# A two-block transformer layer in float32 on one core: the low part of the three weight sums of the feed-forward input made by an accumulating DMA

## The reference, cut to what matters

```
D_MODEL = 2048
SEQ = 256
D_FF = -(-8 * D_MODEL // (3 * 256)) * 256
...
        h = rms_norm(x, norm_ffn[l])
        gate_up = jnp.einsum('btd,df->btf', h, w_ffn_in[l])
        ff_gate, ff_up = jnp.split(gate_up, 2, axis=-1)
        x = x + jnp.einsum('btf,fd->btd', jax.nn.silu(ff_gate) * ff_up, w_ffn_out[l])
```

## Time and profile before

| | us |
|---|---|
| median of 3 runs | 2148.68 |
| lowest, highest | 2147.15, 2149.55 |
| span of the profiled execution | 2146.8 |
| shortest run less that span | 0.35 |
| median less that span | 1.9 |
| TensorE busy | 2135.6 (99%) |
| VectorE busy | 1742.5 (81%) |
| ScalarE busy | 1261.2 (59%) |
| GpSimd busy | 138.1 (6%) |

### The profile page before, as it was taken

One profiled execution on the slowest core, in us unless ns is written; L12 is line 12 of the kernel. 1 busy time (PEld: TensorE's weight loads), 2 busy tenths in 40 slices (PEclk: granted clock), 3 DMA queues, 4 the chain that ended last, 5 costly groups with the idle time before them and its releaser, 6 DMA issues.

```text
span 2146.8 us, 30208 instructions
## 1 busy us (share of the span) xinstructions
PE 2135.6 (99%) x10176; PEld 1788.8 (83%) x10176; DVE 1742.5 (81%) x2125; ACT 1261.2 (59%) x1483; POOL 138.1 (6%) x218
## 2 busy tenths in 40 slices
PE   9999999999999999999999999999999999999998
PEld 9988888888888888888888888888888888888886
DVE  6578788666565698999899887787889999999886
ACT  6465455465544665555555555557667666666565
POOL 2022433101000000000000000000000000000000
PEclk9999999999999999999999999999999999999999
DMA  7666555575555566666666666666666666656664
GB/s 254 182 189 211 157 157 150 174 236 174 183 186 181 186 205 199 198 196 198 203 188 196 200 193 199 192 204 187 206 206 187 188 193 194 193 180 208 203 193 152
DMA packets 211513, 412.35 MB, mean 192 GB/s; under 512 B 13176, under 2 KB 13280, under 8 KB 211296
## 3 DMA queue, kind: packets, MB, share of 16 engines
q1 hardware_dynamic: 208608, 402.70, 60.9%
q0 software_dynamic: 1920, 5.31, 0.8%
q10 hardware_dynamic: 896, 3.15, 0.5%
HBM read 409.01 MB, written 3.16 MB: 192 GB/s over the span
## 4 chain that ended last, share of the span: by engine, by line
PE 96%; DVE 2%; DMA 1%; ACT 0%; issue 0%; DVEq 0%; SPq 0%; ACTq 0%
PE gp L1983 49%; PE gp L1915 33%; PE mx L1983 10%; PE mx L2226 1%; PE mx L2110 1%; DVE w_lo L1194 1%; DMA raw<-a_w_out_in 1%; PE mx L2275 1%; DVE t_lo L1426 0%; DVE ff_lo L1193 0%; PE mx L2113 0%; DMA x_tok<-x_in 0%; PE mx L2107 0%; PE mx L2162 0%; PE mx L2206 0%
## 5 line engine op out<-in xcount | busy, mean ns | idle before, releaser
L615 ACT ACTIVATE w_hi<-raw 128x1024 fp32r<-128x1024 f32 x759 | 797.1, 1056 | 681.6 <-PE gp L1915 246.3
L1194 DVE TENSOR_TENSOR w_lo<-raw,w_hi 128x1024 fp32r<-128x1024 f32 x759 | 921.2, 1230 | 233.8 <-ACT w_hi L615 224.1
L1983 PE MATMUL gp<-w_hi,a_hi 128*128 128x512 f32 x1053 | 413.3, 393 | 0.0
L1983 PE MATMUL gp<-w_lo,a_hi 128*128 128x512 f32 x1053 | 410.1, 389 | 0.0
L1983 PE MATMUL gp<-w_hi,a_lo 128*128 128x512 f32 x1053 | 409.8, 389 | 0.0
L1983 PEld LDWEIGHTS gp<-w_hi,a_hi 128*128 128x128 f32 x1053 | 197.7, 188 | 43.0 <-issue 2.9
L1983 PEld LDWEIGHTS gp<-w_lo,a_hi 128*128 128x128 f32 x1053 | 197.6, 188 | 41.4
L1983 PEld LDWEIGHTS gp<-w_hi,a_lo 128*128 128x128 f32 x1053 | 197.8, 188 | 39.8
L1915 PE MATMUL gp<-w_hi,a_hi 128*128 128x512 f32 x576 | 229.9, 399 | 0.0
L1915 PE MATMUL gp<-w_lo,a_hi 128*128 128x512 f32 x576 | 224.6, 390 | 0.0
L1915 PE MATMUL gp<-w_hi,a_lo 128*128 128x512 f32 x576 | 224.3, 389 | 0.0
(11 more groups left out here) (420 smaller groups left out, 3305.3 us busy)
## 6 DMA issues: line engine op xcount, KB each, us to landing
raw<-a_w_in_in SPq DMA_DIRECT2D x192, 512.0 KB, 4.5
raw<-w_ffn_in_in SPq DMA_DIRECT2D x176, 512.0 KB, 4.5
raw<-w_in_in SPq DMA_DIRECT2D x175, 512.0 KB, 3.9
raw<-w_ffn_out_in SPq DMA_DIRECT2D x88, 512.0 KB, 4.6
raw<-a_w_out_in SPq DMA_DIRECT2D x64, 512.0 KB, 4.9
raw<-w_out_in SPq DMA_DIRECT2D x32, 512.0 KB, 4.0
raw<-w_proj_a_in SPq DMA_DIRECT2D x16, 512.0 KB, 4.6
raw<-w_proj_b_in SPq DMA_DIRECT2D x16, 512.0 KB, 4.7
```

The source lines that it names most:

```text
L615: act.activation(w_hi[:, slot], raw[:, slot], ACT.Copy).then_inc(hi_ready, 1)
L1194: dve.tensor_tensor(w_lo[:, slot], raw[:, slot], w_hi[:, slot], ALU.subtract).then_inc(lo_ready, 1)
L1983: ins = pe.matmul(out_, stat[sp_], mov[mp], start=start and p == 0, stop=stop and p == 2, skip_group_check=True)
```

## The change

In stage FFN_IN alone, VectorE no longer writes `t_lo`. ScalarE writes the negated high part into `t_lo` with a second activation behind `t_hi` (Copy with scale -1). GpSimd waits for it and issues one DMA from `t_sum` to `t_lo` that adds to what the destination holds: `t_lo` = -high + sum. It does so 32 times, on the semaphore `t_added`. TensorE's wait before the last nine matmuls, and VectorE's before it overwrites `t_sum`, are on `t_added` in this stage. The other stages keep their subtraction; `lows` only corrects their counts. No transfer is issued by hand elsewhere, and the shapes stay.

```diff
@@ -429,6 +431,18 @@
+        added_pairs = len(MIXED_FIRST) + (S[FFN_IN].steps - 1) * len(MIXED)
+
+        def added(i, n):
+
+            if isinstance(i, int) and i == 0:
+                return 16 * n
+            return i * (16 * len(MIXED)) + 16 * (n + len(MIXED_FIRST) - len(MIXED))
+
+        def lows(k, i, n):
+
+            return pairs(k, i, n - (added_pairs if k > FFN_IN else 0))
+
@@ -587,6 +601,9 @@
             pool.dma_start(ws_raw[:], a_w_s.rearrange("g p q -> p g q")).then_inc(ws_in, 16)
+            for n in range(added_pairs):
+                pool.wait_ge(t_neg_ready, n + 1)
+                pool.dma_start(t_lo[:].bitcast(F32), t_sum[:], accum_op=ALU.add).then_inc(t_added, 16)
             pool.wait_ge(ws_turned, 1)
@@ -744,6 +761,8 @@
                     act.activation(t_of(k)[1][:], t_of(k)[0][:], ACT.Copy).then_inc(t_hi_ready, 1)
+                    if k == FFN_IN:
+                        act.activation(t_lo[:], t_sum[:], ACT.Copy, scale=-1.0).then_inc(t_neg_ready, 1)
@@ -1395,8 +1414,12 @@
-                if not (isinstance(i, int) and pairs(k, i, n) == 0):
-                    dve.wait_ge(t_lo_ready, pairs(k, i, n))
+                if k == FFN_IN and not (isinstance(i, int) and added(i, n) == 0):
+                    dve.wait_ge(t_added, added(i, n))
+                if k == FFN_OUT and n == 0 and i == 0:
+                    dve.wait_ge(t_added, 16 * added_pairs)
+                elif k != FFN_IN and not (isinstance(i, int) and lows(k, i, n) == 0):
+                    dve.wait_ge(t_lo_ready, lows(k, i, n))
@@ -1421,7 +1444,7 @@
-                if u in mixed(k, i) and half == 1:
+                if u in mixed(k, i) and half == 1 and k != FFN_IN:
                     dve.wait_ge(t_hi_ready, pairs(k, i, mixed(k, i).index(u) + 1))
@@ -2061,7 +2084,10 @@
-                pe.wait_ge(t_lo_ready, pairs(k, i, n + 1))
+                if k == FFN_IN:
+                    pe.wait_ge(t_added, added(i, n + 1))
+                else:
+                    pe.wait_ge(t_lo_ready, lows(k, i, n + 1))
```

More of the change, by code:

```diff
@@ L259, in build @@
         t_lo_ready = sem("t_lo_ready")
+        t_neg_ready = sem("t_neg_ready")
+        t_added = sem("t_added")
         t_used = sem("t_used")
```

## The result

The changed kernel takes 2314.39 us (median; lowest 2312.47) against 2148.15: ratio 1.0772, 95% interval 1.0755 to 1.0789. 166 us slower; the forecast was 2351, 202 slower, with 2225 to 2490 as its range. One of the four executions of the changed kernel took 2724.41 us at a mean granted clock of 0.75, where the other three have 0.97 to 0.98, so the ratio is from the three (2312.47 to 2315.72, median 2313.06). The profile is of the one of 2315.72.

A forecast was written before the change was run, and what follows sets the result against it. TensorE, always busy in FFN_IN, was taken as the bound. Removed work 0, first-pair stalls 66, following-pair stalls 118 and clock 18 made 202 us; on the 2146.8 span 2349, plus 1.9 to the median, 2351; range 2225 to 2490.

The forecast's parts named there:

- VectorE's 56 us: FFN_IN: removing 32 subtractions of 1758 ns saves 56.3 us of VectorE, under an always busy TensorE, so worth nothing.
- X: FFN_IN, each of 32 pairs: time from the end of ScalarE's negation to TensorE's release by the adding DMA.
- X - 3.0: Stall at the first pair of each of 11 steps of FFN_IN: 6.0 us each, 66 us.
- X - 3.4: Stall at 21 following pairs, with releases 6.8 + X apart in place of 10.20: 5.6 us each, 118 us.
- The margin of 3.05 us: Following pairs of FFN_IN: the negation ends 3.05 us before TensorE's need, so X up to that causes no stall.
- The `ff` copy behind the negation: ScalarE, u = 2 of steps 1 to 10: copy moved by 1.38 us, TensorE at least 0.6 late, ten times, 6 us.
- X = 9.0: Adding DMA: 1.9 us fixed, 3.8 for reading 1573 KB, 3.8 for weight loads beside it, some 0.5 taken off.
- the likeliest case: Whole kernel: X between 8 and 10.2, time 2319 to 2393 us, likeliest 2351; chance 0.42.
- the rival of a copy's price: Adding DMA costs what a copy does, X 5 to 8: 2280 us at 7.1, 2230 at 5.8; chance 0.28.
- An add is paid by what it reads: Adding DMA: it reads sums and destination, 1573 KB at 410 GB/s, 3.8 us; a copy 1.9.
- The clock, 18 us at first pairs and none elsewhere: TensorE restarts at half speed after a stall: 1.84 us at ten next steps' first pairs, 18 us; free at following pairs.
- 184 us of idle TensorE: FFN_IN: TensorE idle before the matmuls needing the add, 32 times, some 184 us in all, by 32 X - 104.

The follow-up runs named there:

- e9: Changed kernel with 12 matmul instructions of zeros ahead of each of TensorE's 32 waits for the add: 2309.19 us, ratio 1.0749.
- e5: Changed kernel with each FFN_IN weight load bringing 128 of 512 columns (128 KB in place of 512): 2262.69 us, ratio 1.0539.
- e2: Changed kernel with the DMA copying the 768 KB of sums over the negated high part in place of adding: 2232.03 us, ratio 1.0395.
- e3: Changed kernel with the DMA adding only the first of three sums (256 KB in place of 768): 2200.31 us, ratio 1.0243.
- e10: Changed kernel with a second buffer of sums for each step's middle pair, so following pairs' sums skip the wait for the add: 2283.28 us, ratio 1.0638.
- e1: Kernel before, with ScalarE's second activation (negation) added and VectorE adding the sums in place of a DMA: 2158.73 us, ratio 1.0049.
- e8: Changed kernel with the DMA adding only 16 columns (8 KB) and FFN_IN weight loads cut to 128 KB: 2158.37 us, ratio 1.0049.
- e6: Changed kernel with 24 matmul instructions of zeros ahead of each of TensorE's 32 waits for the add: 2332.22 us, ratio 1.0858.
- e11: Changed kernel with a second buffer of sums for the middle pair and the negation ahead of the high part: 2284.07 us, ratio 1.0637.

## Why the prediction was right, and where it was off

- **TensorE waits for nothing before; VectorE's 56 us are worth nothing.** Right. VectorE is 54 us less busy and nothing is faster: from the release of the stage's last pair to the end it is 952 us, before 951.
- **Every pair stalls, first pairs by X - 3.0, following by X - 3.4.** Right. The rule holds over five values of X at following pairs: 5.0 against 5.1 (e9), 4.8 against 4.7 (change), 3.1 against 3.2 (e5), 2.2 against 2.3 (e2), 1.4 against 1.5 (e3). X is measured in each, so this tests the loop of 6.8 + X, and not the size of X; releases were to be 15.8 us apart and are 15.0. It holds because both TensorE's and VectorE's wait are in the loop, which e10 shows by taking one out.
- **The margin of 3.05 us.** Right: in e1, where no transfer is waited for, the negation ends 2.98 us ahead of the matmul in the mean of the following pairs. The very first pair has less, since its sums start only 8.1 us ahead of the need, 1.5 us of margin; with an X of 9.1 it was costed like the others at 6.0 and cost 7.6.
- **The `ff` copy behind the negation.** Right in mechanism; 0.96 each (e1), where 0.6 was given as the least.
- **X = 9.0.** This is the mis-sized term. Measured, 8.0 in the mean: 0.3 to hand over, 2.0 for a small add from its issue (e8), 4.1 for the bytes (e5 less e8), 1.3 for three quarters of the weight loads' bytes (after less e5), so some 1.7 for all of them as an estimate in proportion. I had 1.9 fixed, 3.8 for the bytes and, with the allowance of 0.5, 3.3 for the loads. Two terms were a little small and the third was about twice too large: I had let every load in flight take its full time from the add. The loads hardly paid for it themselves (landing 4.7 in place of 4.5). At X = 8.0 the formula gives 152, not 184. The measured time is 5 us below the span given for the likeliest case (2319 to 2393; at X = 10.2 its upper end comes to 2389), and X = 8.0 lies on the border to the rival of a copy's price. The time alone would not have told the two apart; e2 does.
- **An add is paid by what it reads.** Right in price within what was tested: 4.2 us above the 8 KB add, a copy 2.1, and 2.4 times the copy's time of the DMA engines. That the reading is the reason stays open, as said at e2. The rival of the copy's price gave 2230 to 2280, and the kernel that really copies (e2) takes 2232, so the rival's time was right for its case.
- **The clock, 18 us at first pairs and none elsewhere.** Right in mechanism, too large in size. First intervals are 1.1 longer than X - 3.0, in e5 0.6, in e2 0.3 and in e3 none, in the order of their stalls; following pairs obey X - 3.4 without it. 11 us, not 18. That it is the clock is shown by the table above, where the 1.1 us are gone in e6 at a clock of 1.00. The price of 1.84 was taken from the kernel's start, where the granted clock reads 1.00 all along, so that row did not show the half clock. In the sum it was near: TensorE's 59 us more busy are 1.9 per pair, most of it hidden in waits.
- **184 us of idle TensorE.** Wrong in form: the idle is 104. I had put idle and slow time together; at half clock, TensorE fills part of its own wait with slower matmuls, which hides most of that loss.
- **The figure of the Trainium skill.** The Trainium skill (DMA: Bandwidth & Descriptors, Anatomy of one DMA) has 2.0 us fixed, which e8 agrees with (2.0). Its rate of 436 GB/s makes an estimate of 1.8 us for 768 KB, near the 1.9 us for which the copy of e2 keeps the 16 engines busy; the add keeps them busy for 4.5, and traffic adds the rest. X was 8.0, not the 3.8 by that formula.

202 forecast, 167 measured on the span: 32 of the difference is X and 7 the clock, while the very first pair gives 2.6 back and the 1.8 us ahead of the stage are in the measurement alone. That X came so near is in part luck: its terms were off in both directions, the loads' by some 1.6 us.

## What to carry to other kernels

Before work goes to a DMA, read from the timeline how long the value lies ready before it is needed, and count in what else waits for the same completion: with 3 us in hand, a transfer of 8 us costs its overshoot every time, and the reuse of its source turns a delay into a loop. Count the bytes of an adding DMA twice: above a small transfer, it took twice as long here as a copy of the same size. A cheap instruction put ahead of others on an idle engine costs by what is queued behind it, and an earlier issue can be lost again to the loads that it then meets.

## What was not expected of the hardware

- The granted clock fell 2.1 us after the last matmul in a wait in the middle of the kernel, and 3.6 us after it at the end; it came back nearly six us after the restart. It fell in 24 of the 32 waits, in one with 2.0 us of idle time and not in another with 3.4.
- The kernel's first 16 matmuls take twice as long as the same 16 later (3.79 and 1.95 us), although the granted clock reads 1.00 in every slice there.
- A small add on GpSimd's queue lands in 3.2 us beside full weight loads and in 2.0 beside quarter loads, so even 8 KB wait 1.2 us in traffic.
- GpSimd's issue of the 768 KB add takes 0.84 us (median of 32), that of the copy of the same shape 0.53; the first packet moves 1.4 us after the start of the issue in both.
- The profile counts the bytes of an adding DMA once, while its engines are busy 2.4 times as long as for a copy. The GB/s of a stretch with adds in it is low for that reason.
- A weight load beside the add took up to 9.0 us to land (e11, where the median is 5.3).
